# Tokens of an attention layer ordered by parity: eight blocks of scores a head instead of nine

## The reference

```python
DILATION_CONFIGS = ((128, 1), (512, 4), (2048, 16))       # (window, dilation), 3 groups of 8 heads
qkv = (h @ w_qkv).reshape(B, S, 3, N_DIL, HEADS_PER_GROUP, HEAD_DIM)
q = apply_partial_rope(qkv[:, :, 0], cos, sin)            # the same for k
# a query t sees the keys t - j*dilation for j = 0 .. window/dilation
for g, (window, dilation) in enumerate(DILATION_CONFIGS):
    o_g, l_g = dilated_group_attention(q[:, :, g], k[:, :, g], v[:, :, g], window, dilation)
wts = jax.nn.softmax(jnp.stack(lses), axis=0)             # merge of the groups by their denominators
o = jnp.einsum('gbsh,gbshe->bshe', wts, jnp.stack(outs))
return o.reshape(B, S, ATTN_WIDTH) @ w_o
```

## Time and profile before

| | |
|---|---|
| median of three runs | 2271.98 us |
| the profiled execution's own time | 2273.46 us |
| its span (first to last instruction) | 2271.7 us |
| PE busy | 2254.0 us, 99% |
| DVE busy | 1482.1 us, 65% |
| ACT busy | 1269.9 us, 56% |
| DMA of the weight stream | 413.43 MB, 56.0% of 16 engines' span |

### The profile page before, as it was taken

One profiled execution on the slowest core, in us unless ns is written; L12 is line 12 of the kernel. 1 busy time (PEld: TensorE's weight loads), 2 busy tenths in 40 slices (PEclk: granted clock), 3 DMA queues, 4 the chain that ended last, 5 costly groups with the idle time before them and its releaser, 6 DMA issues.

```text
span 2271.7 us, 38101 instructions
## 1 busy us (share of the span) xinstructions
PE 2254.0 (99%) x13098; PEld 2000.2 (88%) x13098; DVE 1482.1 (65%) x1764; ACT 1269.9 (56%) x1587; POOL 105.9 (5%) x85
## 2 busy tenths in 40 slices
PE   9999999999999999999999999999999999999998
PEld 7888888888888888888888888888888888888887
DVE  6578676666766655556666666686766667665443
ACT  6455466666666634444555555556666666654443
POOL 4122100000000000000000000020000000000000
PEclk9999999999999999999999999999999999999999
DMA  7644565555555555555555555555555565556563
GB/s 263 198 155 158 185 199 189 190 189 191 187 185 191 189 193 189 190 188 197 167 167 172 169 167 173 170 167 185 192 187 192 186 190 187 187 192 191 189 190 134
DMA packets 115477, 419.21 MB, mean 185 GB/s; under 512 B 12832, under 2 KB 12960, under 8 KB 115168
## 3 DMA queue, kind: packets, MB, share of 16 engines
q1 hardware_dynamic: 114192, 413.43, 56.0%
q0 software_dynamic: 512, 2.95, 0.3%
q10 hardware_dynamic: 720, 2.10, 0.3%
HBM read 416.33 MB, written 2.10 MB: 184 GB/s over the span
## 4 chain that ended last, share of the span: by engine, by line
PE 96%; POOL 1%; ACT 1%; DVE 1%; issue 0%; DMA 0%; DVEq 0%; SPq 0%; ACTq 0%; POOLq 0%
PE acc L1033 61%; PE acc L1034 32%; POOL vsum L406 1%; POOL ssum L381 0%; PE sc_ps L1178 0%; PE sc_ps L1158 0%; PE sc_ps L1165 0%; DMA raw<-w_stream 0%; PE acc L1221 0%; PE sc_ps L1173 0%; PE sc_ps L1157 0%; PE misc L1149 0%; ACT X L567 0%; ACT w_hi L443 0%; ACT U L605 0%
## 5 line engine op out<-in xcount | busy, mean ns | idle before, releaser
L1033 PE MATMUL acc<-X,w_hi 128*128 128x512 f32 x4480 | 1566.1, 392 | 4.8 <-DVE w_lo L733 2.7
L733 DVE TENSOR_TENSOR w_lo<-raw,w_hi 128x1024 fp32r<-128x1024 f32 x784 | 968.3, 1242 | 517.2 <-ACT w_hi L443 516.9
L1034 PE MATMUL acc<-X,w_lo 128*128 128x256 f32 x4480 | 1264.2, 282 | 0.0
L443 ACT ACTIVATE w_hi<-raw 128x1024 fp32r<-128x1024 f32 x784 | 824.9, 1058 | 448.8 <-PE acc L1034 437.6
L1033 PEld LDWEIGHTS acc<-X,w_hi 128*128 128x128 f32 x4480 | 842.4, 188 | 181.2 <-DVE w_lo L733 3.4
L1034 PEld LDWEIGHTS acc<-X,w_lo 128*128 128x128 f32 x4480 | 848.2, 189 | 0.5
L1033 PE MATMUL acc<-hid,w_hi 128*128 128x512 f32 x1408 | 488.2, 390 | 0.0
L1034 PE MATMUL acc<-hid,w_lo 128*128 128x256 f32 x1408 | 397.1, 282 | 0.0
L1033 PEld LDWEIGHTS acc<-hid,w_hi 128*128 128x128 f32 x1408 | 264.3, 188 | 55.4
L1034 PEld LDWEIGHTS acc<-hid,w_lo 128*128 128x128 f32 x1408 | 266.1, 189 | 0.0
L453 ACT ACTIVATE hc<-acc 128x512 f32<-128x512 f32 x104 | 62.0, 596 | 156.7 <-PE acc L1034 156.7
(11 more groups left out here) (141 smaller groups left out, 1066.6 us busy)
## 6 DMA issues: line engine op xcount, KB each, us to landing
raw<-w_stream SPq DMA_DIRECT2D x784, 512.0 KB, 3.5
out<-out_sb SPq DMA_DIRECT2D x8, 256.0 KB, 2.9
h<-x_t ACTq DMA_DIRECT2D x3, 512.0 KB, 10.1
WS<-ws_t POOLq DMA_DIRECT2D x1, 1024.0 KB, 5.3
BS<-bs_row POOLq DMA_DIRECT2D x1, 1024.0 KB, 8.3
mask<-mask_d POOLq DMA_DIRECT2D x1, 576.0 KB, 4.4
h<-x_t ACTq DMA_DIRECT2D x2, 256.0 KB, 5.1
rope<-rope_d POOLq DMA_DIRECT2D x1, 256.0 KB, 3.0
```

The lines of the kernel that those rows point to most:

```text
L443: nc.scalar.activation(w_hi[slot][:, :], raw[slot][:, :], ACT.Copy).then_inc(hi_ready, 1)
L733: nc.vector.tensor_tensor(w_lo[slot][:, :], raw[slot][:, :], w_hi[slot][:, :], ALU.subtract)\
L1033: nc.tensor.matmul(bank, hi, moving[:, kt, :], start=first, stop=False)
L1034: op = nc.tensor.matmul(bank[:, S:2 * S], lo, moving[:, kt, 0:S], start=False, stop=last)
```

## The change

The tokens of the attention layer are ordered by parity: the 128 even ones first, then the 128 odd ones. The order is made where `X`, `rinv` are written for norm 2 (source read with a step of two elements, result written without a step), in the host's tables for rotary factors and mask, and undone where `OX` is written (read without a step, written with a step of two elements, 8 bytes). `h` stays in the order of the tokens.

With even queries in the first half and odd ones in the second, group 0 needs all four blocks of scores (every query half sees keys of both halves), and groups 1 and 2 need two blocks each (own parity alone): eight blocks, in two parts of 512 columns instead of 384 and 768. `attend` uses each v block of group 0 for both query halves in one matmul of 256 columns, whose moving operand is two pieces of 128 columns of `pt` (512 columns apart).

```diff
-Q0 = GROUPS * P
-SC = Q0 + GROUPS * S
+Q0 = S + (GROUPS - 1) * P
+SC = 2 * Q0
+def by_parity(ap):
+    return ap.rearrange("p (i r) -> p r i", r=2)
+def parities(ap):
+    return ap.rearrange("p (r i) -> p r i", r=2)
...
-        Q1 = 512
-        score_parts = ((0, Q0, 0), (Q0, SC, Q1))
+        score_parts = ((0, Q0, 0), (Q0, SC, Q0))
... norm_pair (ACT, high part of X)
+                    to, source = X[:, 2 * pr + b, 0:S], h[:, 2 * pr + b, :]
+                    if n == 2:
+                        to, source = parities(to), by_parity(source)
+                    nc.scalar.activation(to, source, ACT.Copy,
... head_out (ACT)
-                nc.scalar.activation(OX[:, h_, 0:S], out_ps, ACT.Copy).then_inc(o_hi, 1)
+                nc.scalar.activation(by_parity(OX[:, h_, 0:S]), parities(out_ps), ACT.Copy).then_inc(o_hi, 1)
... x_low (DVE, low part of X)
+                    to, source, high = X[:, 2 * pr + b, S:2 * S], h[:, 2 * pr + b, :], X[:, 2 * pr + b, 0:S]
+                    if n == 2:
+                        to, source, high = parities(to), by_parity(source), parities(high)
... head_out (DVE)
-                nc.vector.tensor_tensor(OX[:, h_, S:2 * S], out_ps, OX[:, h_, 0:S], ALU.subtract)\
-                    .then_inc(o_ready, 1)
+                nc.vector.tensor_tensor(by_parity(OX[:, h_, S:2 * S]), parities(out_ps), by_parity(OX[:, h_, 0:S]),
+                                        ALU.subtract).then_inc(o_ready, 1)
... scores (PE)
                 for g in range(GROUPS):
-                    q, k = QK[par][:, g, 0, :], QK[par][:, g, 1, :]
-                    nc.tensor.matmul(sc_flat[:, P * g:P * (g + 1)], q[:, 0:P], k[:, 0:P], start=True, stop=True)
-                    op = nc.tensor.matmul(sc_flat[:, Q1 + S * g:Q1 + S * (g + 1)], q[:, P:S], k, start=True, stop=True)
+                    for t in range(2):
+                        q = QK[par][:, g, 0, P * t:P * (t + 1)]
+                        a, b = (0, S) if g == 0 else (P * t, P * (t + 1))
+                        c = Q0 * t + (S + P * (g - 1) if g else 0)
+                        op = nc.tensor.matmul(sc_flat[:, c:c + b - a], q, QK[par][:, g, 1, a:b], start=True, stop=True)
... attend (PE)
-                for g in range(GROUPS):
-                    nc.tensor.matmul(out_ps[:, 0:P], VT[par][:, g, 0, :], pt[:, P * g:P * (g + 1)],
-                                     start=(g == 0), stop=(g == GROUPS - 1))
-                for g in range(GROUPS):
-                    for n in range(2):
-                        c = Q0 + S * g + P * n
-                        op = nc.tensor.matmul(out_ps[:, P:S], VT[par][:, g, n, :], pt[:, c:c + P],
-                                              start=(g == 0 and n == 0), stop=(g == GROUPS - 1 and n == 1))
+                both = pt[:, :].rearrange("p (t c) -> p t c", t=2)
+                for n in range(2):
+                    nc.tensor.matmul(out_ps, VT[par][:, 0, n, :], both[:, :, P * n:P * (n + 1)], start=(n == 0), stop=False)
+                for t in range(2):
+                    for g in range(1, GROUPS):
+                        op = nc.tensor.matmul(out_ps[:, P * t:P * (t + 1)], VT[par][:, g, t, :],
+                                              both[:, t, S + P * (g - 1):S + P * g], start=False,
+                                              stop=(t == 1 and g == GROUPS - 1))
```

More of the change, by code:

```diff
@@ L462, in norm_pair @@
                 for b in range(2):
-                    nc.scalar.activation(X[:, 2 * pr + b, 0:S], h[:, 2 * pr + b, :], ACT.Copy,
+                    to, source = X[:, 2 * pr + b, 0:S], h[:, 2 * pr + b, :]
+                    if n == 2:
+                        to, source = parities(to), by_parity(source)
+                    nc.scalar.activation(to, source, ACT.Copy,
                                          scale=vecs[:, one(GAINS[n] + 2 * pr + b)]).then_inc(x_hi, 1)
@@ L742, in inverse_rms @@
                 dve.wait_ge(rms_ready, n + 2)
-                nc.vector.reciprocal(rinv[:, :], std[:, :]).then_inc(rinv_ready, 1)
+                to, source = rinv[:, :], std[:, :]
+                if n == 2:
+                    to, source = parities(to), by_parity(source)
+                nc.vector.reciprocal(to, source).then_inc(rinv_ready, 1)
                 dve.wait_ge(rinv_ready, n + 1)
@@ L748, in x_low @@
                     dve.wait_ge(x_hi, KT * n + 2 * pr + b + 1)
-                    nc.vector.scalar_tensor_tensor(X[:, 2 * pr + b, S:2 * S], h[:, 2 * pr + b, :],
-                                                   vecs[:, one(GAINS[n] + 2 * pr + b)], X[:, 2 * pr + b, 0:S],
+                    to, source, high = X[:, 2 * pr + b, S:2 * S], h[:, 2 * pr + b, :], X[:, 2 * pr + b, 0:S]
+                    if n == 2:
+                        to, source, high = parities(to), by_parity(source), parities(high)
+                    nc.vector.scalar_tensor_tensor(to, source, vecs[:, one(GAINS[n] + 2 * pr + b)], high,
                                                    ALU.mult, ALU.subtract).then_inc(x_ready, 1)
@@ L1323, in rope_table @@
     table[2 * HALF:3 * HALF, 1] = np.sin(ang)
-    return table
+    return table[:, :, np.concatenate([np.arange(0, S, 2), np.arange(1, S, 2)])]
 def mask_table():
@@ L1331, in mask_table @@
         for window, dilation in DILATIONS:
-            dist = (P * qt + np.arange(P))[:, None] - np.arange(P * (qt + 1))[None, :]
+            keys = [np.arange(r, S, 2) for r in range(2) if dilation % 2 or r == qt]
+            dist = np.arange(qt, S, 2)[:, None] - np.concatenate(keys)[None, :]
             seen = (dist >= 0) & (dist <= window) & (dist % dilation == 0)
```

## The result

The changed kernel takes 2268.93 us, the median of 20 runs (2268.72 to 2270.61), beside 2272.87 us for the kernel before in the same measurement (20 runs, 2270.29 to 2273.80). The ratio is 0.9986, with a 95% interval from 0.9980 to 0.9992: faster by 0.14% (the two medians alone differ by 3.9 us, 0.17%). The forecast was 2267.4 us with a range from 2266.0 to 2270.2. The time lies in the range, 1.5 us above the forecast. The profiled execution took 2268.83 us, its span is 2267.1 us.

The account below looks back on a forecast made before the run. The prediction took PE, busy 99% of the span, as the bound. Per head 0.21 + 0.11 + 0.25 = 0.57 us, eight heads 4.6 us, gave 2271.98 - 4.6 = 2267.4 us, range 2266.0 to 2270.2.

Parts of the forecast that it names:

- Scores: Attention scores of a head: one 256-column matmul replaced by one of 128, 0.21 us less, bounds 0.20 and 0.22.
- Transposes: Attention transposes of a head: nine become eight, 0.11 us less.
- Product: Attention product of a head: nine 128-column matmuls become four of 128 and two of 256, 0.25 us less, bounds 0.22 and 0.26.
- Steps of two elements: ACT and DVE accesses to h, std and OX with 8-byte steps: claimed as fast as unstepped ones, costing nothing.
- k = 1: k multiplies a stepped instruction's unstepped duration; 1 means no slowdown, and X at the layer's start costs nothing up to 1.86.
- What becomes late next: Other engines, chains and loads around the attention heads: nothing near becomes late, with transposes 1.9 us and product 4.0 us ahead.
- The sum 4.6: Saving over eight attention heads at 0.57 us each: 4.6 us, from 4.2 to 4.7.
- two nearly equal halves: Chance 0.81 of saving 4.2 to 4.9 us, split at 4.5 us (about 0.2%): 0.43 beyond, 0.38 short.
- Price by the instruction: Rival: matmul price goes by instruction, not columns; 0.78 us saved a head, 6.2 us in all, 2265.8 us; chance 0.06.
- Two pieces at half pace: Rival: attention product's two-piece operand streams at half pace; 0.30 us a head lost, 2274.4 us; chance 0.04.
- Slow steps: Rival: stepped accesses at X and OX slow enough to make the kernel slower, 2273.0 us at k = 4; chance 0.05.
- The saving that does not arrive: Rival: PE gets ahead and meets the weight stream or a split; at most half lost, 2269.7 us; chance 0.04.

Follow-up runs that it names:

- experiment 11: Changed kernel with the mask's HBM tensor at its old 1152 columns, plus twelve filling matmuls for two TensorE waits (vsum, X); 2265.20 us, ratio 0.9966.
- experiment 12: Kernel before the change with the same twelve filling matmuls and nothing else; 2269.89 us, ratio 0.9989.
- experiment 7: Changed kernel with one score matmul and one transpose done twice and the attention product as nine 128-column matmuls; 2273.76 us, ratio to before 1.0007.
- experiment 8: Changed kernel without steps of two elements: X, rinv and OX accessed unstepped, mask and rotary table still in parity order; 2268.73 us, ratio 0.9983.
- experiment 9: Changed kernel with steps of eight float32 elements (32 bytes) instead of two in X, rinv and OX; 2269.45 us, ratio 0.9988.
- experiment 1: Changed kernel run again with no edit; 2268.8 us, ratio 0.9985.
- experiment 2: Changed kernel with the mask's tensor in HBM kept at its old 1152 columns, the last 128 not loaded; 2267.15 us, ratio 0.9977.
- experiment 6: Changed kernel with the rotary table's tensor in HBM 64 KB larger by columns not loaded, mask tensor as changed; 2268.82 us, ratio 0.9983.
- experiment 10: Changed kernel with the attention product's two 256-column matmuls reading contiguous columns of pt instead of two pieces; 2267.46 us, one run.

## Why the prediction was right, and where it was off

- **What bounds the kernel.** Right: PE's work alone. The layer became 4.70 us shorter in the first pair of profiles (4.77 without half clock, experiments 11 and 12), and 4.7 us lie between the medians of experiments 11 and 12. Putting the block back on PE alone (experiment 7) gave all of it back, 495.31 us for the layer.
- **Prices.** Scores: I took 0.21 less, 0.22 was measured. Transposes 0.11, measured 0.11. Product: I took 0.25 from the scores' price of a 256-column matmul, measured 0.26, the upper bound, which came from the mean square's price. Together 0.59 a head instead of 0.57, eight heads 4.7 instead of 4.6 us. (Two quotients are off in their last digit without effect: 1.97 / 3 is 0.657 and not 0.655, and 2.01 / 9 is 0.2233.)
- **Steps of two elements.** Right with k = 1, nearly: on ScalarE 380 ns for 363 at `OX` and 0.95 us for 0.91 at the last pair of X (k about 1.05), on VectorE no difference; no wait at the layer's start, and the wait for `OX` stayed at 0.9. The rule of the Trainium skill (SBUF — State Buffer, section on the DMA port swizzle) that two hits in a line of 16 bytes suffice agrees with experiments 8 and 9: an instruction took at most 17 ns longer at 8 bytes, and 0.2 to 0.3 us longer at 32.
- **What becomes late next.** Right inside the layer. The step that failed is one sentence, which puts a term at nothing: the mask's load "is smaller by a ninth and off the path". The load is off the path, but with the mask's tensor of 1024 columns the output at the very end lands 1.5 us later (experiments 1, 2 and 6), by a mechanism that stays open. The sum 4.6 had to be 4.7 - 1.5 = 3.2 us on equal levels of the clock: 2272.0 - 3.2 = 2268.8, where most runs of the changed kernel lie.
- **The median.** I took 2271.98 as the level, and two runs 0.1 us apart as a sign that it is one; it is the middle of three. In the 20 runs of before, ten lay on the upper one, in the 20 of after five, which is why the medians differ by 3.9 us and not by 3.2; why the shares differ is not shown. Of the forecast's two nearly equal halves, beyond and short of 0.2%, the second came. That the time lies in the range is in part luck: no term of the sum stood for the end, and its 1.5 us used up room that was left for a higher level, lost savings or slow steps.
- **The clock.** The prediction reads "full in every slice" from the earlier trace rows. A digit of 9 there means 90% or more of a slice of 57 us, and before had two stretches of 3.4 us at half clock behind it. They are what the levels are made of.
- **Rivals.** Price by the instruction: excluded, 0.86 us for two matmuls of 256 and 0.89 for four of 128. Two pieces at half pace: excluded by 0.86 us in the changed kernel, and by experiment 10. Slow steps: not at two elements. The saving that does not arrive: it arrived on PE in full, and a third was spent at another place, while this rival had looked for the loss in the weight stream or a split.

## What to carry to other kernels

Where one engine is busy for 99% of the span, a removed instruction of it is worth its start-to-start time, and eight small savings can be summed to a tenth of a microsecond. But compare two profiles mark by mark from start to end, not by their spans: here 1.5 us of clock at the start and 1.5 us of output at the end hid each other, and an input table that became smaller went with a slower landing of the output. And if a kernel's times fall on levels, look for stretches of half clock behind the waits of TensorE, in windows of a few us, since a coarse slice hides them. Work that takes the place of the wait cost nothing here and removed them, be it added at the wait or ahead of it. Look in the trace where an added instruction stands: half of the filling matmuls stood 22 us ahead of the wait that they were meant for.

## What the runs showed of the hardware

- After waits of 1.8 to 2.1 us of an otherwise busy TensorE the granted clock fell to half for 3.4 us, in some executions: in 11 of 12 profiles behind the wait for X, in 2 of 12 behind that for vsum, in 10 of 13 behind that for `w_lo` at 26 us. Such a stretch cost 1.6 us (the layer takes 490.43 us with it in experiment 2, 1530.65 - 1041.81 = 488.84 without it in experiment 10), and nothing at 26 us, where PE waits again otherwise. After waits of 0.7 and 0.8 us for X (experiments 11 and 12), 0.9 us for `OX`, 1.1 us for `GX` and 1.2 and 1.5 us for `w_lo` it did not fall in any profile. Twelve filling matmuls at two places (1.3 us each) brought a spread of 1.6 to 3.5 us over the runs down to 0.4.
- Eight output DMAs of 256 KB landed in 2.9 to 3.0 or in 4.0 us in the median, by the width of an unrelated input tensor in HBM (1152 and 1280, or 1024 float32 columns of 128 rows), in seven profiles each. Another tensor 64 KB smaller or larger did not change it. The cause is open.
- ScalarE and VectorE take 8 bytes between float32 elements at nearly full speed (380 ns for 363 on ScalarE, 418 in both on VectorE), and 32 bytes at about 1.5 to 1.9 times the duration (682 ns for 363 and 662 for 418 at `OX`, 1.50 us for 0.91 and 1.53 for 0.99 at a pair of X).
- For true float32, a moving operand of two pieces of 128 columns, 512 columns apart, cost the same as one of 256 contiguous columns: 0.86 us for two matmuls in both (experiment 10).
